# Two transformer blocks on one core: the feed-forward norm moved to the evictions, merge units interleaved, the short down unit moved to the end, and streamed matmuls dealt out by step

## The reference, cut to what matters

```
x  = first_block input, 512 tokens x 1024
q_mla, k_mla, v_mla           -> o_mla  = causal_attention, 8 heads        (the "first attention")
dq, dk, dv                    -> o_diff = rmsnorm(o1 - lam * o2)           (the "second attention")
gates  = sigmoid(gate_pre + b_gate);  g_mla, g_diff = halves of gates
merged = g_mla * (o_mla @ w_branch_mla) + g_diff * (o_diff @ w_branch_diff)
x      = x + merged @ w_out
hn     = x * rsqrt(mean(x * x) + eps) * norm_ffn_g
hid    = silu(hn @ w_ffn_gate) * (hn @ w_ffn_up)                           # 1024 -> 2816
x      = x + hid @ w_ffn_down                                              # 2816 -> 1024
x      = rmsnorm(x, norm_final_g)
second block: rmsnorm, projections, windowed attention, spatial gating, gates, w_o, rmsnorm
```

## Time and profile before

| what | value |
|---|---|
| median of 3 executions | 1326.67 us (1326.3 to 1327.29) |
| profiled execution, its own time | 1326.54 us |
| its span | 1324.8 us |
| PE busy | 1284.2 us, 97% of the span |
| DVE busy, ACT busy | 669.1 us (51%), 539.1 us (41%) |
| mean granted PE clock | 0.992 of full speed |

### The profile page before, as it was taken

How to read it: one execution, slowest core, us unless ns; L and a number is a source line. 1 busy time by engine, 2 the same in 40 slices (tenths; PEclk the granted TensorE clock), 3 DMA queues, 4 the chain that set the end, 5 groups by cost and what they waited for, 6 DMA issues and landing times.

```text
span 1324.8 us, 15797 instructions
## 1 busy us (share of the span) xinstructions
PE 1284.2 (97%) x6228; PEld 1069.8 (81%) x6228; DVE 669.1 (51%) x1014; ACT 539.1 (41%) x905; POOL 58.6 (4%) x97
## 2 busy tenths in 40 slices
PE   8999999999998999999999999999999999999997
PEld 6877778878877888888888778888988888888885
DVE  6775877644545333333342248845553335435554
ACT  5545665652334343434333134426553334223222
POOL 0001341210000000000000000000000000000000
PEclk9999999999999999999999999999999999999999
DMA  5232112123432323232322322431114332232221
GB/s 192 68 95 65 32 48 64 49 64 95 150 105 64 98 93 106 84 117 77 124 95 80 125 66 64 127 111 33 33 33 143 96 95 96 95 95 96 86 90 64
DMA packets 104428, 116.39 MB, mean 88 GB/s; under 512 B 13423, under 2 KB 88237, under 8 KB 104365
## 3 DMA queue, kind: packets, MB, share of 16 engines
q1 hardware_dynamic: 104240, 115.49, 27.5%
q10 hardware_dynamic: 124, 0.03, 0.0%
HBM read 113.42 MB, written 2.10 MB: 87 GB/s over the span
## 4 chain that ended last, share of the span: by engine, by line
PE 88%; DVE 6%; ACT 3%; issue 2%; POOL 1%; DVEq 0%; ACTq 0%; POOLq 0%
PE ps_mm L1812 56%; PE ps_mm L1847 20%; PE ps_o L2161 2%; PE ps_o L1997 1%; DVE w_lo L1105 1%; PE ps_s L1974 1%; PE ps_t L2141 1%; PE ps_mm L1818 1%; PE ps_mm L1905 1%; ACT w_hi L609 1%; PE ps_s L2018 1%; PE ps_o L2040 1%; PE ps_s L2126 1%; PE ps_s L2124 1%; DVE w_lo L1114 0%
## 5 line engine op out<-in xcount | busy, mean ns | idle before, releaser
L1812 PE MATMUL ps_mm<-act_hi,w_hi 128*128 128x512 f32 x944 | 371.9, 394 | 2.1 <-DVE w_lo L1114 1.5
L1812 PE MATMUL ps_mm<-act_hi,w_lo 128*128 128x512 f32 x944 | 370.6, 393 | 0.0
L1812 PE MATMUL ps_mm<-act_lo,w_hi 128*128 128x512 f32 x944 | 370.5, 392 | 0.0
L1105 DVE TENSOR_TENSOR w_lo<-stage,w_hi 128x2048 fp32r<-128x2048 f32 (+3 forms) x77 | 157.7, 2048 | 189.4 <-ACT w_hi L609 189.3
L1812 PEld LDWEIGHTS ps_mm<-act_hi,w_hi 128*128 128x128 f32 x944 | 177.7, 188 | 37.6 <-DVE w_lo L1114 1.9
L1812 PEld LDWEIGHTS ps_mm<-act_hi,w_lo 128*128 128x128 f32 x944 | 177.6, 188 | 35.3
L1812 PEld LDWEIGHTS ps_mm<-act_lo,w_hi 128*128 128x128 f32 x944 | 177.6, 188 | 34.9
L609 ACT ACTIVATE w_hi<-stage 128x2048 fp32r<-128x2048 f32 (+3 forms) x78 | 134.0, 1719 | 161.8 <-PE ps_mm L1847 117.8
L1504 DVE TENSOR_TENSOR w_lo<-stage,w_hi 128x2048 fp32r<-128x2048 f32 x23 | 52.7, 2292 | 104.2 <-ACT w_hi L891 104.2
L1847 PE MATMUL ps_mm<-w_hi,act_hi 128*128 128x512 f32 x240 | 94.3, 393 | 1.9 <-issue 1.9
L1847 PE MATMUL ps_mm<-w_lo,act_hi 128*128 128x512 f32 x240 | 94.1, 392 | 0.0
(11 more groups left out here) (367 smaller groups left out, 1848.8 us busy)
## 6 DMA issues: line engine op xcount, KB each, us to landing
stage<-in_w_in SPq DMA_DIRECT2D x44, 1024.0 KB, 5.3
stage<-in_w_ffn_gate SPq DMA_DIRECT2D x11, 1024.0 KB, 5.4
stage<-in_w_ffn_up SPq DMA_DIRECT2D x11, 1024.0 KB, 5.4
stage<-in_w_ffn_down SPq DMA_DIRECT2D x10, 1024.0 KB, 5.0
stage<-in_w_out SPq DMA_DIRECT2D x4, 1024.0 KB, 5.0
stage<-in_w_att_out SPq DMA_DIRECT2D x4, 1024.0 KB, 5.0
stage<-in_w_sg_out SPq DMA_DIRECT2D x4, 1024.0 KB, 5.0
stage<-in_w_o SPq DMA_DIRECT2D x4, 1024.0 KB, 5.0
```

Source lines behind the costliest of these rows:

```text
L1105: V.tensor_tensor(w_lo[:, s, 0:k * w], stage[:, s, 0:k * w], w_hi[:, s, 0:k * w].bitcast(F32), ALU.subtract).then_inc(w_lo_made, 1)
L1812: ins = T.matmul(ps_mm[:, 2 * bank_slot + m, :], wt[:, kk, m * P:(m + 1) * P], acts[ap][:, kk, :], start=(r == 0), stop=(r == per - 1), sk ...
```

## The change

Four parts, all in one diff.

1. **First attention.** The weights of `MLA_STREAM` are no longer equal: after three start values they are 5, 4, 2, 4 for p % 4 = 0 to 3 and 5 in the last three steps. The matmuls per step were 6 (5 in two steps); they become 8 or 7, 6, 3, 6 or 7, and 7, 8, 8 at the end. The steps at which a bank is full move from 15, 19, 23, 27, 31 to 16, 20, 24, 28, 32, and the second and third unit start one step later (11 and 19 for 10 and 18).
2. **Merge.** The order becomes gate, merge, gate, merge, gate, merge, merge; the merged activations are split into buffers of their own (`mg_hi`, `mg_lo`), and the subtractions are taken out of the wait for ACT by moving them one unit later.
3. **Feed-forward norm.** `res` is transposed unscaled (columns 0 to 511 in the middle of the third `out` unit, the others token by token inside the fourth and the first gate unit), split with the gain, and `rstd` is applied to every gate and up bank as it is evicted, by a row `xr_b` spread with four transposes. DVE evicts the gate banks too; Silu reads and writes `sl`. `keep_warm(6)` is gone. For each pass of the loop DVE gets four operations of 128x512 more and ACT none.
4. **Down.** `DOWN_K = (4, 4, 4, 4, 4, 2)`.

```diff
-DOWN_K = (2, 4, 4, 4, 4, 4)
+GATE_B = [U0["gate_b"]] + [U0["merge"] + i for i in (0, 2, 4)]
+MRG_D = [U0["merge"] + i for i in (1, 3, 5, 6)]
+DOWN_K = (4, 4, 4, 4, 4, 2)
...
-MLA_STREAM = Stream(U0["dk"], [48] * 4, [0, 0, 1] + [2] * (MLA_STEPS - 3))
+MLA_STREAM = Stream(U0["dk"], [48] * 4, [0, 0, 2] + [(5, 4, 2, 4)[p % 4] for p in range(3, 4 * MH)] + [5] * LAG)
...
@@ ACT, merge
             for i in range(1, 4):
-                hi(U0["gate_b"] + i + 1)
+                hi(GATE_B[i] + 1)
                 for m in range(2):
-                    gate_bank(U0["gate_b"] + i, m, 8 + 2 * i + m)
+                    gate_bank(GATE_B[i], m, 8 + 2 * i + m)
+                hi(MRG_D[i - 1] + 1)
+                if i < 3:
+                    for m in range(2):
+                        merge_hi(2 * i - 2 + m)
+            hi(MRG_D[3] + 1)
+            for c in range(4, 8):
+                merge_hi(c)
...
@@ ACT, out units and norm
+            hi(U0["out"] + 1)
+            hi(U0["out"] + 2)
+            for t in range(TT):
+                ffn_squares(0, t)
+            hi(U0["out"] + 3)
+            for k in range(4):
+                norm_hi_chunk("norm_ffn_g", KD, k)
+            hi_at(uf, uf % 2, lc[uf % 2], 8, 256)
+            for t in range(3):
+                ffn_squares(1, t)
+            norm_hi_chunk("norm_ffn_g", KD, 4)
+            ffn_squares(1, 3)
+            for k in range(5, KD):
+                norm_hi_chunk("norm_ffn_g", KD, k)
...
@@ ACT, loop
-                    nc.scalar.activation(sl[:, m, :], ps_mm[:, 2 * (gf % 2) + m, :], ACT.Silu
-                                         ).then_inc(bank_free_act, 1)
+                    act.wait_ge(bank_free, j * 4 + freed(uf, m))
+                    nc.scalar.activation(sl[:, m, :], sl[:, m, :], ACT.Silu).then_inc(silu_made, 1)
...
@@ DVE, after the out units
+            for k in range(4, KD):
+                norm_lo_chunk("norm_ffn_g", KD, k)
+            dve.wait_ge(norm_squared, TT + 8)
+            add_parts()
+            rsqrt(TT, 1.0 / D, made=2)
+            lo_at(uf + 1, (uf + 1) % 2, 8, 256)
+            dve.wait_ge(xr_turned, 2)
+            after(link(V.tensor_copy(xr_b[:, :], ps_o[:, :])))
+            def ffn_pair(j):
+                for m in range(2):
...
+                    V.tensor_tensor(sl[:, m, :], ps_mm[:, 2 * (gf % 2) + m, :], xr_b[:, :], ALU.mult
+                                    ).then_inc(bank_free, 1)
                 lo_at(j * 2 + (uf + 2), uf % 2, 8, 256)
                 for m in range(2):
...
+                    V.tensor_tensor(tmp[:, m, :], ps_mm[:, 2 * ((gf + 1) % 2) + m, :], xr_b[:, :], ALU.mult
                                     ).then_inc(bank_free, 1)
+                    dve.wait_ge(silu_made, j * 2 + (m + 1))
+                    V.tensor_tensor(sl[:, m, :], sl[:, m, :], tmp[:, m, :], ALU.mult).then_inc(h_made, 1)
                     dve.wait_ge(h_hi_made, j * 2 + (m + 1))
                     V.tensor_tensor(h_lo[:, bass.ds(j * 2 + m, 1), :], sl[:, m:m + 1, :],
...
@@ PE
+            for i in range(1, 4):
+                straight(GATE_B[i], "F", acts_x)
+                if i == 1:
+                    pe.wait_ge(od_made, DH)
+                straight(MRG_D[i - 1], "F", (od[:, :, 0, :], od[:, :, 1, :]))
+            straight(MRG_D[3], "F", (od[:, :, 0, :], od[:, :, 1, :]))
...
+                wide_unit(U0["out"] + i, (mg_hi, mg_lo), token_done=(None, None, turn_first, turn_last)[i])
-            keep_warm(6)
-            turn_chunks(n_sc, 1, KD)
...
+            unit(uf, uf % 2, gf % 2, lambda m: bank_due(gf, m), "F", 8, 256, acts_x, chunk_waits=(norm_lo, KD),
+                 begin_chunk=turn_rest)
+            pe.wait_ge(rstd_made, 2)
+            for t in range(TT):
+                ins = T.transpose(ps_o[:, t * P:(t + 1) * P], rstd[:, t:t + 1].broadcast_to([P, P]), ident[:, :])
+            ins.then_inc(xr_turned, 1)
```

More of the change, by code:

```diff
@@ L65 @@
 COUNTS = [("lat", 3), ("dv", 2), ("qn", 2), ("qp", 1), ("kn", 2), ("mv", 1), ("dk", 2), ("dq", 2),
-          ("gate_m", 8), ("gate_b", 4), ("mrg_d", 4), ("out", 4), ("ffn", 22), ("down", 12),
+          ("gate_m", 8), ("gate_b", 1), ("merge", 7), ("out", 4), ("ffn", 22), ("down", 12),
           ("q2", 4), ("kv2", 1), ("za", 4), ("zs", 4), ("u2", 4), ("vs", 4), ("ga", 4), ("att", 4), ("gs", 4),
@@ L874, in _, with merge_hi @@
                     hi(u + 1)
+            def merge_hi(c):
+                act.wait_ge(merged, c + 1)
+                nc.scalar.activation(mg_hi[:, c, :], gates[:, c, :], ACT.Copy, scale=0.5).then_inc(merged_hi, 1)
             for i in range(1, 4):
-                hi(U0["gate_b"] + i + 1)
+                hi(GATE_B[i] + 1)
                 for m in range(2):
-                    gate_bank(U0["gate_b"] + i, m, 8 + 2 * i + m)
[L882 to L887, removed]
+                    gate_bank(GATE_B[i], m, 8 + 2 * i + m)
[6 more added lines that the diff above has]
+                merge_hi(c)
             def hi_at(u, s, count, k, w):
@@ L895, in _, with ffn_squares @@
             lc = {uf % 2: landed_count(uf - 2) + 16, (uf + 1) % 2: landed_count(uf - 1) + 16}
[L897 to L909, removed]
+            def ffn_squares(n, t):
+                act.wait_ge(bank_free, freed(U0["out"] + 2 * n + 1, t))
+                if t >= 2 or n:
+                    act.wait_ge(norm_squared, TT + 4 * n + t - 1)
+                part_squares(n, t, 0, res, tmp[:, t % 2, :], norm_squared)
+            hi(U0["out"] + 1)
[12 more added lines that the diff above has]
+                norm_hi_chunk("norm_ffn_g", KD, k)
             with act.Fori(0, KF // 2) as j:
@@ L1080, in _ @@
                         act.wait_ge(x_gained, 12 + t + 1)
[L1081 removed]
+                        half_scale(t // 2, 4 + t // 2, res, vs, fin_made_act)
         @block.vector
@@ L1538, in _ @@
                                     ).then_inc(h_lo_made, 1)
+                dve.wait_ge(h_lo_made, j * 2 + 2)
+            ffn_pair(0)
+            with dve.Fori(1, KF // 2) as j:
+                lo_at(j * 2 + (uf + 1), (uf + 1) % 2, 8, 256)
+                ffn_pair(j)
             ud = U0["down"]
@@ L1561, in _ @@
                                               op0=ALU.mult, op1=ALU.add)))
-            rsqrt_of(8, made=4)
+            rsqrt_of(8, made=3)
             scale_tiles(n_sc, act_y, 4)
@@ L1853, in wide_unit @@
                         ins.then_inc(first_bank_full, 1)
+                    if token_done is not None and kk == k - 1:
+                        token_done(t)
             acts_x = (act_hi, act_lo)
@@ L2051, in _, with turn_token, turn_first, turn_last @@
             for i in range(1, 4):
-                straight(U0["gate_b"] + i, "F", acts_x)
-            pe.wait_ge(od_made, DH)
-            for i in range(4):
-                straight(U0["mrg_d"] + i, "F", (od[:, :, 0, :], od[:, :, 1, :]))
+                straight(GATE_B[i], "F", acts_x)
[3 more added lines that the diff above has]
+            straight(MRG_D[3], "F", (od[:, :, 0, :], od[:, :, 1, :]))
+            def turn_token(u, t, ks):
+                pe.wait_ge(bank_free, freed(u, t))
+                for k in ks:
+                    if t == 0 and k >= 4:
+                        pe.wait_ge(norm_lo, KD + k - 3)
+                    ins = T.transpose(side_bank(k)[:, t * P:(t + 1) * P], res[:, t, k * P:(k + 1) * P], ident[:, :])
+                    if t == TT - 1:
+                        ins.then_inc(norm_turned, 1)
+            def turn_first(t):
+                if t == 1:
+                    for tt in range(TT):
+                        turn_token(U0["out"] + 1, tt, range(4))
+            def turn_last(t):
+                if t:
+                    turn_token(U0["out"] + 3, t - 1, range(4, KD))
             for i in range(4):
```

97 lines of the change are left out of this document (54 added, 43 removed).

## The result

The changed kernel takes 1318.51 us (median of 5 runs, 1316.82 to 1320.32); the kernel before took 1326.52 beside it (1323.73 to 1327.29). The ratio is 0.9942, with a 95% interval of 0.9932 to 0.9953: 8 us faster. The forecast was 1317.5, in a range of 1312.3 to 1322.3. The profiled execution of the changed kernel took 1318.19 us, with a span of 1316.3.

A forecast was written before the change was run, and what follows sets the result against it. PE was taken to bound the kernel, 88% of the chain, so only its waits could pay. -2.2 - 4.0 - 5.9 - 1.7 + 3.2 + 1.4 = -9.2 from 1326.67 gave 1317.5 us, range 1312.3 to 1322.3.

The forecast's parts named there:

- the attention: First attention: the last query split moves behind the last copy and its wait goes, -2.2 us; bounds -5.6 and +2.6.
- the merge stage: Merge units: wait before the first `out` unit gone, two new waits of 0.2 us, -2.4; with the clock -4.0.
- the down products: Down units: both successors of short units now follow full units, so their waits of 0.5 and 1.2 us go, -1.7.
- the loss in the tail: Behind the last down product: evictions bunch up, +3.2 us, and longer idling lowers the clock, +1.4 us.
- I take these two as cancelling: First attention rounds: query splits before a shorter copy against less cover in 3-matmul steps, together no gain or loss.
- the missing cover of the 3-matmul steps: First attention: 3 matmuls (0.68 us) must cover a 0.61 us copy plus signals; if exposed in seven steps, +2.6 us.
- The clock term of 1.6: Merge: closing the 1.94 us gap before the first `out` unit also removes the low clock behind it, -1.6 us.
- Norm: Between the last `out` matmul and the loop: all but PE's own work goes behind matmuls, -5.9 us; bounds -6.5 and -2.0.
- The 0.3 us set down for that wait: Start of the loop: PE waits for the first up unit's split, ready 12.2 us after the unit's end against 12.0.
- Loop: Feed-forward loop: DVE's added work costs 0 behind PE; the chain grows from 7.0 to 7.8 us under 10.9 of cover.
- The rival in which the loop falls behind: Feed-forward loop: the up-bank chain outgrows its cover and PE waits in ten passes, +10 us and more; chance 0.05.
- a short idle stretch is free: Clock behind down before the change: 1.8 us idle after the warming matmuls kept clock 1.00, so costs nothing.

The follow-up runs named there:

- att_undone: The changed kernel with the old, even dealing of streamed weights in the first attention; 1317.74 us, ratio 0.9934.
- merge_undone: The changed kernel with three gate units and then four merge units again, merged activations keeping their own buffers; 1320.90 us, ratio 0.9955.
- loop3: The changed kernel with three more unused DVE reductions of the second up bank in each loop pass; 1318.72 us, ratio 0.9938.
- loop6: The changed kernel with six more unused DVE reductions of the second up bank in each loop pass; 1328.57 us, ratio 1.0013.
- warm39: The changed kernel with 39 warming matmuls behind the down units instead of 18; 1316.63 us, ratio 0.9926.
- down_mid: The changed kernel with the short down unit third in each half, DOWN_K = (4, 4, 2, 4, 4, 4); 1314.39 us, ratio 0.9904.

## Why the prediction was right, and where it was not

- **The sum** was -9.2; the profiled executions differ by 8.35 and the medians by 8.0. That is closer than the terms were, and in part luck. The gain was put 2.0 us too high for the attention and 0.6 for the merge stage. It was put 0.9 too low for the stretch of `out`, norm and loop and 0.5 for the down products, and the loss in the tail 0.3 too high. (The lower end of the range is added up wrong: 1317.5 less 3.4 and 1.4 is 1312.7, not 1312.3. Nothing hangs on it.)
- **Attention: wrong.** The failed step is "I take these two as cancelling". -2.2 was forecast; the stage is 0.5 us shorter by its own length and ends 0.25 earlier. The end of the stage came as said: the split moved behind the last copy and its wait went. But I followed one query split only, the last. The others moved too, each into the step ahead of an eviction of `ps_o`, and the waits for `om_lo` rose from 1.6 to 3.5 us. I had named the eviction and the half splits ahead of it, and then looked for the cost of the query splits only against the copy `pt`. att_undone shows the whole part to be worth 0.5 us in the traces and nothing that the medians can tell. That the missing cover of the 3-matmul steps costs anything did not show either: there is no wait for `pt` in the changed kernel.
- **Merge: right in its mechanism.** The gap is gone, and two new waits of 0.2 us stand where they were forecast, 0.5 in all by the view of waits. Each costs 0.5 us with the restart behind it, though (11.19 us for the next 48 matmuls instead of 10.92), and the 0.6 us more than forecast is the whole difference between -2.4 and -1.8. The clock term of 1.6 was the price of an event that doesn't come each time. The part measured 2.4 by merge_undone, against 4.0 forecast, within the bounds of 1.5 and 4.6.
- **Norm: right.** -6.2 measured alone, -5.9 forecast. The split of the first up unit ends at 424.48, and PE comes to it at 424.77. The 0.3 us set down for that wait were not needed. The difference of the two traces gives -6.7 (8.4 less 1.7 of clock): beside its products PE has 3.9 us of transposes there, where 3.9 and 0.45 and 0.3 were set down.
- **Loop: right,** with DVE busy 113.1 us over the whole loop (about 111 forecast), 7.8 us of chain, and a cover that loop3 and loop6 bracket. The rival in which the loop falls behind had a chance of 0.05; it stood 3.1 us of chain away, and its price beyond the limit was put too low by half.
- **Down: right.** Both waits went (-2.2 with the restarts, -1.7 forecast). The fourth bank's squares start 3.75 us after the last product (4.0 forecast), and the clock fell behind the longer idle time (4.7 us by the view of waits), at 1.4 us by warm39, as forecast. The part as a whole was a loss, some 2 us in the table above where the prediction's own terms gave 2.9; its two halves could be had apart, as down_mid shows.
- **The clock behind a gap: right at one place, too sure at the other.** Behind down, with 4.7 us idle, it fell in all six traces that have this idle time. Behind the 1.94 us before the first `out` unit it fell in two of three (0.57, 0.57 and 1.00 in the same 4 us), and the prediction took that one as certain. The Trainium skill ("TensorE: Matmul & The Clock Gate", What's actually happening) calls the number of slow matmuls before the clock rises run-variable for one and the same kernel; it does not say that of the fall behind a gap. No more do the traces bear out "a short idle stretch is free" as a rule: the 1.8 us behind the warming matmuls kept clock 1.00 in all seven traces that have them, 1.94 us elsewhere did not.

## What to carry to other kernels

When units are dealt out anew, follow every operation that hangs on a full bank, not only the one whose wait you want to be rid of: each stands in some in-order list ahead of something that frees a buffer. A short unit is best put between full ones: it still covers the split of its successor when nothing else stands in front of that split, but not the evictions of the stage before as well, and as the last one it makes the evictions bunch up where nothing follows. Before latency is added to a pipelined loop, measure from the full bank to the operand needed: below the cover it costs nothing, and half a microsecond beyond it costs a whole one in every pass. When two traces are compared, compare lengths of stages and not ends, or a shift from earlier is read as an effect.

## What the runs showed of the hardware

Low stretches of the clock (granted clock 0.50 in windows of 1 us) came at some places of the program in every trace and at others only in some. The full-clock time lost in one, added up over windows of 1 us, was about 1.7, 3.4 or 5.1 us. In the fourteen traces:

| place | low stretch in | full-clock time lost, us |
|---|---|---|
| 58 to 63 us, the same program in all | 6 of 14 | 1.7 |
| 101 to 110 us, start of the first attention | 12 of 14 (not loop3, warm39) | 1.7 in nine, 3.4 in three |
| behind the 1.9 us gap before the first `out` unit | 2 of 3 (not merge_undone) | 1.7 |
| hand-off before the loop, norm as before the change | 2 of 2 | 1.7 and 3.4 |
| behind down, short unit last and 18 warming matmuls | 6 of 6 | 1.7 in two, 3.4 in two, 5.1 in two |
| behind down in all other kernels | 0 of 8 | |
| end of the program | 14 of 14 | not added up |

That is as large as the differences that I was to explain. It makes much of the spread between runs of one kernel, for every run has its mean granted clock on record. Of the 39 executions of the kernel before beside the experiments, four have a clock of 0.995 and took 1323.4 to 1323.5 us; the others have 0.992 to 0.994 and took 1326.1 to 1328.5. In loop6 the six at 0.994 or 0.995 took 1326.3 to 1328.7 us, the four at 0.991 or 0.992 1329.2 to 1330.9. As an estimate, 0.002 of the clock over a span of 1325 us is 2.7 us.

A wait of 0.2 us at PE costs about 0.3 us more than its length: the 48 matmuls behind it take 11.19 us, where a unit that follows another without a wait takes 10.92. The first of them starts 0.62 us after the matmul before it, the second 0.34 after the first, instead of 0.23.

On the loop's chain stands a reload of ACT's function tables, between the copy `h_hi` and the split of the next weights (ACT's timeline in the changed kernel):

```profile
459.15 0.63 ACT L943 ACTIVATE h_hi<-sl 128x512 f32 x1 [4.81 <-DVE sl L1580]
459.80 1.28 ACT L905 ACT_TABLE_LOAD   x1
461.09 1.92 ACT L905 ACTIVATE w_hi<-stage 128x2048 fp32r<-128x2048 f32 x1
```

It is 1.28 of the 7.8 us, ahead of a plain copy (`ACT.Copy`). The Trainium skill ("ScalarE: Activation LUTs", Table sets: the hidden batching unit) says that cheap functions such as the copy are in every set; by that rule this load would be needless. The trace agrees so far that the other weight copy of the pass (447.89, L905) follows a Silu (447.36, L938) without a load. To do without this one was not tried.
